# Wide attention scores as rounded passes, two norm chains planned later, and the mixer's weight lows moved to VectorE

## The reference

```python
def mla_block(qn_blk, qr_blk, kn_pre, kr_pre, v_pre, t0):
    s = (jnp.einsum('bqhd,bkhd->bhqk', qn_blk, kn_pre)      # d = 128
         + jnp.einsum('bqhr,bkr->bhqk', qr_blk, kr_pre)).astype(jnp.float32) * MLA_SCALE   # r = 64
    s = jnp.where(causal, s, jnp.finfo(jnp.float32).min)
    p = jax.nn.softmax(s, axis=-1)
    return jnp.einsum('bhqk,bkhd->bqhd', p.astype(v_pre.dtype), v_pre)
...
mixed = jnp.concatenate([rmsnorm(o_sb, sb_out_norm_g[l]), rmsnorm(o_mla, mla_out_norm_g[l])], axis=-1)
h = h + jnp.einsum('bse,ed->bsd', mixed, w_o[l])
```

## Time and profile before

| what | value |
|---|---|
| median of 3 runs | 3112.85 us (3111.34 to 3117.41) |
| the profiled execution | 3111.43 us, span 3109.6 us |
| PE busy | 2967.6 us, 95% of the span |
| DVE, ACT, POOL busy | 56%, 39%, 25% |

### The profile page before, as it was taken

One profiled execution on the slowest core, in us unless ns is written; L12 is line 12 of the kernel. 1 busy time (PEld: TensorE's weight loads), 2 busy tenths in 40 slices (PEclk: granted clock), 3 DMA queues, 4 the chain that ended last, 5 costly groups with the idle time before them and its releaser, 6 DMA issues. The chain is left out here.

```text
span 3109.6 us, 39823 instructions
## 1 busy us (share of the span) xinstructions
PE 2967.6 (95%) x15577; PEld 2318.2 (75%) x15577; DVE 1729.9 (56%) x2297; ACT 1210.4 (39%) x1847; POOL 777.8 (25%) x412
## 2 busy tenths in 40 slices
PE   8998999999999999999899999999999999999997
PEld 6675555778887888777677777777777788877885
DVE  4566756564554222655468667666565333347856
ACT  4345644343333112444553334333444333533233
POOL 1110002235442222442121001012111344421233
PEclk9999999999999999999999999999999999999998
DMA  4221000242335222342421111114323223456643
GB/s 154 92 89 68 8 18 1 91 149 92 111 110 223 89 96 101 127 169 98 125 98 62 48 66 55 65 55 142 110 99 104 97 101 113 167 192 227 233 149 129
DMA packets 145441, 335.95 MB, mean 108 GB/s; under 512 B 12392, under 2 KB 53608, under 8 KB 145128
## 3 DMA queue, kind: packets, MB, share of 16 engines
q1 hardware_dynamic: 118184, 268.65, 25.4%
q10 hardware_dynamic: 27072, 64.76, 5.3%
HBM read 234.80 MB, written 97.52 MB: 107 GB/s over the span
## 5 line engine op out<-in xcount | busy, mean ns | idle before, releaser
L2294 PE MATMUL psum<-normed_hi,w_hi 128*128 128x512 f32 x984 | 423.0, 430 | 10.2 <-ACT buffer L1942 5.4
L2773 POOL TENSOR_TENSOR w_lo<-raw,w_hi 128x1024 fp32r<-128x1024 f32 x64 | 172.9, 2702 | 918.4 <-ACT w_hi L1942 918.4
L2296 PE MATMUL psum<-normed_hi,w_lo 128*128 128x512 f32 x984 | 387.7, 394 | 0.0
L2295 PE MATMUL psum<-normed_lo,w_hi 128*128 128x512 f32 x984 | 386.6, 393 | 0.0
L1477 POOL TENSOR_TENSOR w_lo<-raw,w_hi 128x1024 fp32r<-128x1024 f32 x79 | 198.6, 2514 | 703.0 <-ACT w_hi L1177 644.4
L2294 PEld LDWEIGHTS psum<-normed_hi,w_hi 128*128 128x128 f32 x984 | 187.1, 190 | 59.4 <-issue 20.6
L2296 PEld LDWEIGHTS psum<-normed_hi,w_lo 128*128 128x128 f32 x984 | 186.2, 189 | 41.5
L2295 PEld LDWEIGHTS psum<-normed_lo,w_hi 128*128 128x128 f32 x984 | 187.5, 191 | 37.4 <-issue 6.5
L1177 ACT ACTIVATE w_hi<-raw 128x1024 fp32r<-128x1024 f32 x79 | 83.6, 1058 | 294.3 <-PE psum L1059 262.0
L1942 ACT ACTIVATE buffer<-psum,par 128x512 f32<-128x512 f32 (+1 forms) x131 | 93.1, 712 | 257.7 <-PE psum L2296 242.9
L1746 DVE TENSOR_TENSOR res<-psum,res 128x512 f32<-128x512 f32 x80 | 55.2, 690 | 213.5 <-PE psum L1059 213.5
(11 more groups left out here) (544 smaller groups left out, 7328.7 us busy)
## 6 DMA issues: line engine op xcount, KB each, us to landing
raw<-in_w_in SPq DMA_DIRECT2D x75, 512.0 KB, 4.3
scratch_in<-buffer ACTq DMA_DIRECT2D x59, 512.0 KB, 2.7
raw<-in_w_mlp SPq DMA_DIRECT2D x42, 512.0 KB, 3.5
scratch_gate<-gate_out ACTq DMA_DIRECT2D x60, 256.0 KB, 2.0
gate_in<-scratch_gate SPq DMA_DIRECT2D x27, 512.0 KB, 4.1
scratch_hid<-hidden_out ACTq DMA_DIRECT2D x44, 256.0 KB, 4.3
split_plain<-scratch_y SPq DMA_DIRECT2D x20, 512.0 KB, 7.3
raw<-in_w_br SPq DMA_DIRECT2D x18, 512.0 KB, 5.0
```

The source lines that it names most:

```text
L2294: pe.matmul(out, hi, xh, start=k == 0, stop=False)
L2295: pe.matmul(out, hi, xl, start=False, stop=False)
L2296: mm = pe.matmul(out, lo, xh, start=False, stop=k == DC - 1)
L2773: pool.tensor_tensor(ws.lo[:, n % 2], raw[:, n % 2], ws.hi[:, n % 2].bitcast(F32), ALU.subtract).then_inc(w_lo, 1)
```

## The change

1. **Wide scores.** For t of 16 and more, `wide_scores` makes nope and rope each in three rounded passes, so six passes for a chunk in place of two float32 matmuls. The wide steps go head by head (block rows 4, 5, 6, 7 of head 0, then of head 1, ...). New splits: ACT makes the highs (`wide_highs`, ten instructions), POOL the lows (`wide_lows`, ten), and DVE two halves of 128x512. The planned length of a wide step changes from 0.7 + 0.76 (b+1) to 0.8 + 0.62 (b+1). The third weight split of the output projection moves from ahead of the steps to step 25.
2. **Last output norm.** For n = 3 the sum on PE is due 2 us earlier, log and exp on ACT 3.4 us later, the highs 3 us later, which puts a weight split between them.
3. **Latent norm.** Its sums, roots and products are due 2 to 3 us later, and the pace of the products behind it is 2.1 in place of 2.2.
4. **Mixer.** Of 64 instructions L2773 on POOL, 63 move to DVE, as a generator of its own in the weave.

```diff
+            def wide_scores(t, b, h, rows, to):
+                n, queries = (b + 1) * P, slice((b - HALF // P) * P, (b - HALF // P + 1) * P)
+                if t == step_of(HALF // P, h):
+                    pe.wait_ge(split_lo, 4 + 2 * h)
+                    if h == 0:
+                        pe.wait_ge(k_rope, 3)
+                nope = Split(qn_hi[h], qn_lo[h])[:, queries]
+                rope = Split(qr_hi[rows, h // 2], qr_lo[rows, h // 2])[:, queries]
+                for c in range(0, n, HALF):
+                    keys = slice(c, min(c + HALF, n))
+                    three_passes(pe, to[:, keys], nope, Split(kn_hi[h], kn_lo[h])[:, keys], True, False)
+                    mm = three_passes(pe, to[:, keys], rope, Split(kr_hi[rows], kr_lo[rows])[:, keys], False, True)
...
-        return rows_order[t // MLA_H]
+        return rows_order[t // MLA_H] if t < T // 2 else HALF // P + t % MLA_H
...
+            def wide_highs():
+                yield step_at[2]
+                act.wait_ge(q_rope, 2)
+                act.wait_ge(k_rope, 1)
+                act.wait_ge(product_done, N)
+                act.activation(qr_hi, qr[:, 0:2, HALF:S], ACT.Copy).then_inc(split_hi, 1)
+                act.activation(kr_hi, kr, ACT.Copy).then_inc(split_hi, 1)
+                for h in range(MLA_H):
+                    yield split_at[h]
...
+                    act.activation(qn_hi[h], halves(qn[:, h])[1], ACT.Copy).then_inc(split_hi, 1)
+                    act.activation(kn_hi[h], kn(h), ACT.Copy).then_inc(split_hi, 1)
...
-                    yield t_out[n] + (5.5 if n < 3 else 9.0)
+                    yield t_out[n] + (5.5 if n < 3 else 7.0)
...
-                    yield t_out[n] + 4.6
+                    yield t_out[n] + (4.6 if n < 3 else 8.0)
...
-                        yield t_out[n] + 7.0 + 0.8 * j
+                        yield t_out[n] + (7.0 if n < 3 else 10.0) + 0.8 * j
...
-                yield T_LOW + 6.0
+                yield T_LOW + 9.0
...
-    gemm_at, gemm_pace = T_LOW + 24.0, 2.2
+    gemm_at, gemm_pace = T_LOW + 26.0, 2.1
...
-            for n in range(1, len(st.slots) - 1):
-                pool.wait_ge(w_hi, n)
-                if n >= 2:
-                    pool.wait_ge(unit_done, st.done_at[n - 2])
-                pool.tensor_tensor(ws.lo[:, n % 2], raw[:, n % 2], ws.hi[:, n % 2].bitcast(F32), ALU.subtract).then_inc(w_lo, 1)
+            pool.wait_ge(w_hi, 1)
+            pool.tensor_tensor(ws.lo[:, 1], raw[:, 1], ws.hi[:, 1].bitcast(F32), ALU.subtract).then_inc(w_lo, 1)
...
+            def weights():
+                for n in range(2, len(st.slots) - 1):
+                    yield pace(st.done_at[n - 2]) + 1.6
+                    dve.wait_ge(w_hi, n)
+                    dve.wait_ge(w_lo, n - 1)
+                    dve.wait_ge(unit_done, st.done_at[n - 2])
+                    dve.tensor_tensor(ws.lo[:, n % 2], raw[:, n % 2], ws.hi[:, n % 2].bitcast(F32), ALU.subtract).then_inc(w_lo, 1)
```

More of the change, by code:

```diff
@@ L451, in in_step @@
         return step_at[t] + share * (step_at[t + 1] - step_at[t])
+    split_at = [step_at[6]] + [step_at[T // 2 + MLA_H * h] + 1.0 for h in range(MLA_H - 1)]
     OUT = [("sb", 0), ("sb", 1), ("mla", 0), ("mla", 1)]
@@ L995, in scores_of_step @@
                 rows, to = slice(64 * (h % 2), 64 * (h % 2) + 64), scores(t)
+                if t >= T // 2:
+                    wide_scores(t, b, h, rows, to)
+                    return
                 for c in range(0, n, HALF):
@@ L1460, in last_roots @@
                         act.activation(halves(xn.hi[:, j])[h], halves(scaled_x[:, j])[h], ACT.Copy).then_inc(u_hi, 1)
-            woven(norm(), norm_roots(), highs(), tables(), stick(), stick_turns(), latent(), outputs(), values(), keys_out(), hidden_units(), corners(), t_scales(), hidden_high(), left_highs(), z_halves(), mlp_highs(), mlp_sums(), mlp_roots(), last_sums(), last_roots(), weights())
+            woven(norm(), norm_roots(), highs(), tables(), stick(), stick_turns(), latent(), wide_highs(), outputs(), values(), keys_out(), hidden_units(), corners(), t_scales(), hidden_high(), left_highs(), z_halves(), mlp_highs(), mlp_sums(), mlp_roots(), last_sums(), last_roots(), weights())
         @block.gpsimd
@@ L1507, in mlp_low @@
                                            ALU.subtract).then_inc(u_odd, 1)
-            woven(outputs(), mlp_low(), left_lows(), weights())
+            woven(wide_lows(), outputs(), mlp_low(), left_lows(), weights())
         @block.vector
@@ L1710, in latent @@
                         dve.wait_ge(l_done, w + 1)
-                        to, (out, inverse) = mo[w % MLA_H][:, b * P:(b + 1) * P], latent_out(w)
+                        to, (out, inverse) = mo[head_of(w)][:, b * P:(b + 1) * P], latent_out(w)
                         dve.tensor_copy(to, out).then_inc(l_copied, 1)
@@ L1899, in last_roots @@
                                               halves(xn.hi[:, j - 1])[h].bitcast(F32), ALU.subtract).then_inc(u_even, 1)
-            woven(norm(), lows(), gemm(), stick_masks(), stick(), stick_out(), latent(), outputs(), tables(), corners(), adds(), hidden_units(), turned_sums(), left_sums(), hidden_low(), mlp_sums(), mlp_lows(), last_sums(), last_roots())
+            woven(norm(), lows(), gemm(), stick_masks(), stick(), stick_out(), latent(), wide_lows(), outputs(), tables(), corners(), adds(), hidden_units(), turned_sums(), left_sums(), hidden_low(), mlp_sums(), mlp_lows(), last_sums(), last_roots())
 def heads(v):
```

102 lines of the change are left out of this document (75 added, 27 removed).

## The result

The changed kernel took 3086.99 us (median of 3 runs, 3083.48 to 3088.49) against 3112.85 before: a ratio of 0.9912, interval 0.9889 to 0.9934. Measured again over six runs, beside 22 of the kernel before, it was 0.9928 (0.9915 to 0.9942), 3090.25 against 3111.44 us. So the change takes off 22 to 27 us. The forecast was 3099, a gain of 13, with a range that ended at 3087. Both profiled executions of the changed kernel (3083.48 and 3083.53 us) are the fastest of their group, 3.5 and 6.7 us under its median, so their traces show a little too much gain. A ratio with its interval is not the quotient of the two medians and can differ from it by some 2 us.

What follows compares the result with a forecast made beforehand. PE, busy 95% of the span, was taken as the bound. Terms -7 + 1 - 4 - 3 + 0 = -13 us on 3111.43 gave 3098.4, 3099.8 in medians, stated as 3099; own range 3092 to 3106, over all cases 3087 to 3110.

Steps and rivals of the forecast that it cites:

- the latent norm's term: Latent norm, 284 to 330 us: stick-breaking matmuls ahead of the sum win half its 5.7 us wait, -3 us.
- The bound of -7 for the whole: Latent norm's best case: the sum's whole wait and one slow clock stretch go, -7 us.
- Wide scores, -7: Wide steps of latent attention: six rounded passes replace two float32 matmuls, -7 us, bounds -19 and +2.
- +1 for the splits: New splits on ACT and POOL in the wide steps make PE wait longer: +1 us, bounds -3 and +5.
- the passes' price: Wide scores: three passes take 0.90 us at 512 keys, 0.73, 0.56 and 0.55 at 384, 256 and 128.
- The rival in which changes of rows cost nothing: Wide scores: switching between 128 and 64 rows is free, gain 19 instead of 7, time 3087; chance 0.10.
- Last norm, -4: Last output norm: PE's wait for w_lo shrinks from 5.66 to 2.2 us, -4 us, bounds -7.5 and -1.
- the walk through POOL's queue: Last output norm: three lows pass before w_lo, which ends at about 592.2, so PE waits 2.2 us.
- Mixer, 0: Mixer: 63 lows moved from POOL to DVE; relief and new waits cancel, 0 us, bounds -6 and +10.
- the chunk chosen: Mixer near 1758 us: DVE's moved low waits for w_hi ahead of the 128x4 copy, which still ends at 1761.0.
- the 759 of a plain sum: Mixer: DVE's busy time forecast as 682 + 77 = 759 of 1120 us.

Runs made afterwards that it cites:

- nope_first: The changed kernel with both nope chunks of a wide step ahead of both rope chunks: 3082.55 us, ratio 0.9903.
- last_norm_alone: The kernel before with only the due times of the last output norm changed: 3103.68 us, ratio 0.9974.
- low_early: The changed kernel with POOL's weight low at the last output norm behind one low of the norm instead of three: 3084.10 us, ratio 0.9907.
- mixer_alone: The kernel before with only the 63 weight lows of the mixer moved from POOL to DVE: 3108.42 us, ratio 0.9987.

## Why the forecast fell short

**The step that failed is the latent norm's term.** The prediction put it at -3: "I take half of L912's wait", because "what PE does earlier it misses later". It measured -8 to -10 us by the last narrow step, and 12 us in time alone. Three things were missing. Less of the wait at the sum came back than half: the stick-breaking matmuls moved ahead of it fill the time in which DVE prepares, and PE's waits up to 330 fell from 16.2 us to 10.9 and 12.0. By waits the norm's due times are worth 4.3 us, so this part of the term was right in kind and 1 us short. The larger miss is that the new due times of the products (26.0 and 2.1) had no term at all, though the diff has them. They took 3.9 us of waits away: the wait for v_latent went from 2.27 to 0.43, and stick-breaking matmuls left from among the products. And 3 to 7 us less ran at the lower clock, worth 2 to 3 us, which the term had in its bound alone. The bound of -7 for the whole was too near.

**Wide scores, -7 with +1 for the splits**: the passes' price was right, the other terms were not, and that the sum of -6 came out is luck. PE's work fell by 0.13, 0.49, 0.48 and 0.57 us in the steps of block rows 4 to 7, 6.7 us over four heads, as the passes' prices said. But waits took back 3.0 in the wide steps and 0.9 in a narrow one, not 1, and the new order and plan gave 2.4 to 2.7, which the prediction had only as a remark. The rule of TensorE: Matmul & The Clock Gate, Part 3, The mechanism, in the Trainium skill, that a load overlaps only when its row group differs, would have made the passes of one group 0.34 us apart; here they are 0.23 apart (535.26 to 535.49 above), so the measurement disagrees with the rule in this case. The same section of the Trainium skill also lets a load go ahead into the background weight buffer, and with that the 0.23 agrees; the prediction had left this out. The rival in which changes of rows cost nothing gave 3087, the time that was measured, by the wrong cause: nope_first shows that a change does cost 0.2 us of PE's work.

**Last norm, -4**: the walk through POOL's queue gave a wait of 2.2 us and the trace has 2.29, 2.0 the second time; half of the slow stretch behind it stayed. From the mask of step 31 to the end of the output projection the two traces gained 4.7 and 4.8 us. The order on POOL was taken as given, and its price was not asked for; last_norm_alone and low_early show that the order on POOL held back 2 to 4 us more.

**Mixer, 0**: PE's waits from the first weight tile to the last are the same within 1 us (48.1 before, 48.9 and 49.1 after), and the chunk chosen came out as walked through, with the low and the convolution instruction ahead of the copy. DVE's 691 us are less than the 759 of a plain sum, because the blocking by POOL's lows is gone, of which the copy's 2.31 us for 0.16 is the one instance shown. The Trainium skill's rule of the exclusive port pair (SBUF — State Buffer, SBUF: two separate sides) agrees with that.

**Sum.** Forecast -3, -6, -4 and 0; measured by landmarks about -9, -5.5, -4.8 and -1 (mixer_alone), together -20, and 22 to 27 in time. The 2 to 7 us between are not tied to a part: they lie behind the output projection, where executions scatter.

## What to carry to other kernels

Cost every number of a planner that a diff touches, a pace as well as a due time: a new start and 0.1 us less of pace for the products took 3.9 us of waits, as much as the rewritten score products gave. When ready work goes ahead of a wait of the bounding engine, follow the waits behind it: here 5.7 us left one place, and 4.2 to 5.3 stayed won. Work taken off an engine that is near its neighbours' pace comes back in part as waits, 3.0 of 6.7 us and 2.4 of 6.4 here. And when two parts of a change move the same queue, read the order again for both together: the last norm gave 7 us alone and 2 to 5 in company, until one due time on POOL was set after it.

## What the runs showed of the hardware

A change between rounded matmuls of 128 rows and of 64 rows costs 0.2 us, half at the leave and half at the entry (0.33 and 0.31 to 0.34 us where 0.23 is the pitch); grouping by rows took two such changes out of each of 16 steps, 6.4 us of PE's work, and won 4.0 us. Three rounded passes beat a plain float32 product at 512 columns (0.87 against 0.95 us with 128 rows) and lose at 128 (0.96 against 0.84 us for nope and rope). A half-clock stretch in the wide steps was worth 2.6 us in the kernel before (105.7 us with it, 103.1 in three kernels without it) and 3.1 in the changed one (100.2 and 97.1). It came or stayed away between kernels that have the same instructions there, so a difference of 3 us between two single executions need not come from the edit.
